# First attention of a two-block network: running sums of probabilities kept in a bank, three score banks, one wide reciprocal, second head's parts and a Fourier table moved later

## The reference

```
def one_block(qblk):
    s = einsum('bqhgd,bkhd->bhgqk', qblk, k) * scale
    p = softmax(s, axis=-1)
    return einsum('bhgqk,bkhd->bqhgd', p, v)
...
yb = blocked_attention(q, k_all, v_all)
y = concatenate([ya * silu(a_gate), yb * silu(b_gate)], axis=-1)
return y @ w_out
```

## Time and profile before

| | us |
|---|---|
| median of 3 runs | 4290.86 (4288.06 to 4292.45) |
| the profiled execution | 4291.51 |
| its span | 4289.7 |
| PE / PEld busy | 4061.0 / 3106.1 |
| DVE / ACT / POOL busy | 2073.7 / 1321.8 / 1532.8 |
| attention and its tail, about 360 to 649 us | 289 |

### The profile page before, as it was taken

The page is one execution under the profiler, slowest core; times in us unless marked ns, Lnnn a source line. Parts: engine busy times, 40 slices in busy tenths (PEclk is TensorE's granted clock), DMA queues, the critical chain, the costliest instruction groups (busy, mean ns, idle before and its releaser), DMA issues.

```text
span 4289.7 us, 49866 instructions
## 1 busy us (share of the span) xinstructions
PE 4061.0 (95%) x19447; PEld 3106.1 (72%) x19447; DVE 2073.7 (48%) x2300; ACT 1321.8 (31%) x1996; POOL 1532.8 (36%) x882
## 2 busy tenths in 40 slices
PE   7998998899999998899999999999999899999998
PEld 5776774457777774578888788876766578888886
DVE  4264883865676775561543233324454654323322
ACT  3123550222222221231332232234455533223222
POOL 0535770111111111122444444434454544444443
PEclk8999999999999999899999999999999999999999
DMA  6110005331122114741233333322000032333333
GB/s 231 38 40 20 1 1 207 128 133 63 66 80 74 70 68 164 179 141 49 89 93 98 98 98 94 102 79 73 22 25 26 16 118 93 98 98 95 96 99 106
DMA packets 118854, 372.15 MB, mean 87 GB/s; under 512 B 18020, under 2 KB 33695, under 8 KB 114912
## 3 DMA queue, kind: packets, MB, share of 16 engines
q1 hardware_dynamic: 98960, 296.38, 22.1%
q0 software_dynamic: 12800, 59.50, 3.9%
q10 hardware_dynamic: 6928, 13.96, 0.9%
HBM read 329.37 MB, written 38.06 MB: 86 GB/s over the span
## 4 chain that ended last, share of the span: by engine, by line
PE 65%; issue 15%; DVE 9%; POOL 6%; DMA 2%; ACT 2%; SPq 1%; POOLq 0%; ACTq 0%; DVEq 0%
PE banks L276 22%; PE banks L3218 6%; POOL w_parts L261 6%; PE banks L1344 6%; PE banks L291 5%; PE banks L696 5%; PE banks L1719 4%; PE banks L3292 2%; PE banks L3321 2%; PE banks L1001 1%; PE banks L3308 1%; PE banks L1700 1%; DMA w_ring<-in_weights 1%; PE banks L1014 1%; PE banks L1750 1%
## 5 line engine op out<-in xcount | busy, mean ns | idle before, releaser
L261 POOL TENSOR_TENSOR w_parts<-w_ring,w_parts 128x1024 fp32r<-128x1024 f32 x344 | 842.7, 2451 | 1089.4 <-ACT w_parts L254 1088.9
L276 PE MATMUL banks<-x_high,w_parts 128*128 128x512 f32 x2944 | 911.5, 390 | 0.0
L254 ACT ACTIVATE w_parts<-w_ring 128x1024 fp32r<-128x1024 f32 x344 | 364.6, 1060 | 1283.6 <-PE banks L276 1274.9
L276 PEld LDWEIGHTS banks<-x_high,w_parts 128*128 128x128 f32 x2944 | 552.7, 188 | 116.6 <-issue 2.1
L276 PE MATMUL banks<-x_low,w_parts 128*128 128x512 f32 x1472 | 572.7, 389 | 0.0
L276 PE MATMUL banks<-hidden_high,w_parts 128*128 128x512 f32 x1600 | 482.9, 392 | 6.0 <-POOL w_parts L261 6.0
L3426 DVE TENSOR_TENSOR_SCAN arena<-arena,flags 128x128 f32<-128x128 f32 (+3 forms) x192 | 248.6, 1308 | 250.5 <-ACT arena L3367 248.5
L276 PEld LDWEIGHTS banks<-hidden_high,w_parts 128*128 128x128 f32 x1600 | 302.6, 189 | 71.0 <-POOL w_parts L261 6.8
L3107 DVE TENSOR_TENSOR hidden_high<-banks,gate_temps 128x512 f32 (+1 forms) x88 | 60.8, 691 | 571.9 <-PE banks L276 571.7
L276 PEld LDWEIGHTS banks<-x_low,w_parts 128*128 128x128 f32 x1472 | 276.3, 188 | 59.3 <-issue 1.9
L1344 PE MATMUL banks<-parts_b,w_ring_low 128*128 128x512 f32 x896 | 304.7, 407 | 13.5 <-DVE resid_low L394 9.7
(11 more groups left out here) (478 smaller groups left out, 6832.2 us busy)
## 6 DMA issues: line engine op xcount, KB each, us to landing
w_ring<-in_weights SPq DMA_DIRECT2D x488, 512.0 KB, 3.6
arena<-in_hy_dft SPq DMA_DIRECT2D x11, 1536.0 KB, 6.2
s_cl<-arena POOLq DMA_DIRECT2D x4, 1152.0 KB, 5.4
resid<-in_xT ACTq DMA_DIRECT2D x2, 2048.0 KB, 26.2
resid<-in_xT POOLq DMA_DIRECT2D x2, 2048.0 KB, 12.7
arena<-in_fn_seq POOLq DMA_DIRECT2D x1, 4096.0 KB, 24.6
resid_spill<-resid POOLq DMA_DIRECT2D x1, 4096.0 KB, 12.7
s_e<-arena POOLq DMA_DIRECT2D x4, 1024.0 KB, 5.0
```

What stands on the lines that cost most here:

```text
L254: nc.scalar.activation(WP[:, g % 2, 0, :], WR[:, (g % RING) * TILE:(g % RING + 1) * TILE], ACT.Identity).then_inc(w_hi, 1)
L261: nc.gpsimd.tensor_tensor(WP[:, g % 2, 1, :], WR[:, (g % RING) * TILE:(g % RING + 1) * TILE], WP[:, g % 2, 0, :].bitcast(F32), ALU.subtrac ...
L276: mm = nc.tensor.matmul(PS[:, bank + h // H, :], w[a][:, k % KB, :], srcs[b][:, k, at + h:at + h + H], start=(first and i + q == 0), stop= ...
```

## The change

- The running sum moves from the SBUF tile `ACCP` to bank 3; only the last of a half's nine sums writes `ACCP`. Scores use three banks (i % 3) and wait for the exponentials of block i - 3.
- `denominator(g)` is one product of ones x `ACCP` (128x512) into bank 4, at s = 3; `spread` and `inverse` are gone. `divided(g - 1)` moves from s = 4 to s = 3 and begins with a reciprocal of the whole bank, 128x512, in place.
- The second head's high parts are made behind blocks 25 (keys) and 28 (values), its low parts behind blocks 26 and 29. The clearing of `SHIFT[1]` on GpSimd moves behind block 2; the first half's scores wait for one `a_sh` count less.
- ScalarE does one exponential of a single column ahead of its wait for the pooling part.
- `turned` counts on a semaphore of its own.
- The parameters' loads come ahead of the Fourier table, and the table is issued when the first f32 tile of the output projection is done.

```
-    a_hi, a_lo, a_mx, a_top, a_rc, a_sh = (sem("a_" + x) for x in ("hi", "lo", "mx", "top", "rc", "sh"))
+    a_hi, a_lo, a_mx, a_top, a_tt, a_sh = (sem("a_" + x) for x in ("hi", "lo", "mx", "top", "tt", "sh"))
...
             def scores(i):
-                if i == 3:
-                    p.wait_ge(pme, 4)
-                if i >= 4:
-                    p.wait_ge(a_p, i - 3)
-                out_ = PS[:, i % 4, :]
+                if i >= 3:
+                    p.wait_ge(a_p, i - 2)
+                out_ = PS[:, i % 3, :]
...
             def denominator(g):
                 p.wait_ge(a_ad, KBL * (g + 1))
                 p.wait_ge(a_top, 4 * min(g + 3, HALVES))
-                if g:
-                    p.wait_ge(a_o, 2 * g)
-                for t in range(4):
-                    mm = nc.tensor.matmul(PS[:, 4, t:t + 1], ACCP[g % 2][:, t * P:(t + 1) * P], ONES[:, 0:1],
-                                          start=True, stop=True)
-                mm.then_inc(a_dn, 1)
-            def spread(g):
-                p.wait_ge(a_rc, g + 1)
                 nc.tensor.matmul(PS[:, 4, :], ONES[:, :], ACCP[g % 2], start=True, stop=True).then_inc(a_dn, 1)
...
@@ act
             queries_high(0)
+            nc.scalar.activation(FLAG[:, 2:3], ONES[:, 0:1], ACT.Exp)
             a.wait_ge(pme, 4)
             values_high(0)
...
-                if i == 0:
+                if i == 25:
                     keys_high(1)
+                if i == 28:
                     values_high(1)
...
@@ dve, summed(i)
                 if b == 1:
-                    if g >= 2:
-                        v.wait_ge(a_dn, 2 * (g - 1))
-                    nc.vector.tensor_tensor(acc, PROB[(i - 1) % 3], PROB[i % 3], ALU.add).then_inc(a_ad, 2)
+                    if g:
+                        v.wait_ge(a_ad, KBL * g)
+                    nc.vector.tensor_tensor(PS[:, 3, :], PROB[(i - 1) % 3], PROB[i % 3], ALU.add).then_inc(a_ad, 2)
                 elif b > 1:
                     v.wait_ge(a_ad, i)
-                    nc.vector.tensor_tensor(acc, acc, PROB[i % 3], ALU.add).then_inc(a_ad, 1)
+                    if b == KBL - 1 and g >= 2:
+                        v.wait_ge(a_dn, g - 1)
+                    nc.vector.tensor_tensor(acc if b == KBL - 1 else PS[:, 3, :], PS[:, 3, :], PROB[i % 3],
+                                            ALU.add).then_inc(a_ad, 1)
...
             def divided(g):
-                v.wait_ge(a_dn, 2 * g + 2)
+                v.wait_ge(a_dn, g + 1)
+                link(nc.vector.reciprocal(PS[:, 4, :], PS[:, 4, :]))
                 v.wait_ge(a_o, 2 * g + 1)
...
                 if s == 3 and g:
-                    inverse(g - 1)
-                if s == 4 and g:
                     divided(g - 1)
...
@@ pool
-            g_.wait_ge(pme, 4)
-            nc.gpsimd.memset(SHIFT[1].bitcast(F32), 0.0).then_inc(a_sh, 1)
             values_low(0, 3)
             for i in range(BLOCKS):
                 prob_low(i)
+                if i == 2:
+                    g_.wait_ge(a_sh, 2)
+                    nc.gpsimd.memset(SHIFT[1].bitcast(F32), 0.0).then_inc(a_sh, 1)
                 if i == 3:
                     queries_low(1)
-                if i == 5:
-                    keys_low(1, 5)
-                if i == 8:
-                    values_low(1, 6)
+                if i == 26:
+                    keys_low(1, 7)
+                if i == 29:
+                    values_low(1, 8)
...
@@ HyPrep.pool
+            S5Prep.params(g)
+            wait_sums(g, EvOut.st, 3)
             g.dma_start(ar(0, 8192, "p (i b t) -> p i b t", i=2, b=8),
                         ins["fn_seq"].rearrange("i (b p) t -> p i b t", p=P)).then_inc(seq_in, 16)
-            S5Prep.params(g)
```

More of the change, by code:

```diff
@@ L948, in parts_made @@
     def parts_made(g):
-        return (2, 4)[g] if g < 2 else g + 5
+        return 2 if g == 0 else g + 3 if g < 4 else g + 5
     def top_bank(g, t):
@@ L987, in turned @@
                     p.wait_ge(a_sh, g + 2)
-                nc.tensor.transpose(PS[0:4, 6, 384:512], TOP[g % 2], IDENT[:, :]).then_inc(a_mx, 1)
+                nc.tensor.transpose(PS[0:4, 6, 384:512], TOP[g % 2], IDENT[:, :]).then_inc(a_tt, 1)
             def scores(i):
@@ L1002, in scores @@
                 if b == 0:
-                    p.wait_ge(a_sh, g + 3)
+                    p.wait_ge(a_sh, g + 3 if g else 2)
                 nc.tensor.matmul(out_, MINUS, SHIFT[g % 2], start=False, stop=True).then_inc(a_s, 1)
@@ L1009, in values @@
                 if b == 0:
-                    p.wait_ge(a_lo, 3 if g < HALVES // N_KV else 6)
+                    p.wait_ge(a_lo, 3 if g < HALVES // N_KV else 8)
                     if g:
@@ L1062, in pe @@
                 values(2 * n + 1)
-                if s == 4 and g:
-                    spread(g - 1)
                 if s == 2 and ahead:
@@ L1067, in pe @@
             denominator(HALVES - 1)
-            spread(HALVES - 1)
         def act(a, link):
@@ L1091, in act @@
                     a.wait_ge(a_ad, i - 2)
[L1092 removed]
+                nc.scalar.activation(PROB[i % 3], PS[:, i % 3, :], ACT.Exp, scale=SCALE0)
                 if i >= 3:
                     a.wait_ge(a_pv, i - 2)
[L1095 removed]
+                nc.scalar.activation(PPARTS[0][i % 3], PS[:, i % 3, :], ACT.Exp, scale=SCALE0).then_inc(a_p, 1)
                 if i % KBL == 0 and i // KBL + 1 < HALVES:
                     queries_high(i // KBL + 1)
[L1098 removed]
+                if i == 25:
                     keys_high(1)
+                if i == 28:
                     values_high(1)
@@ L1112, in top @@
             def top(g, t):
-                v.wait_ge(a_mx, 5 * g + t + 1)
+                v.wait_ge(a_mx, 4 * g + t + 1)
                 nc.vector.reduce_max(TOP[g % 2][:, t:t + 1],
@@ L1118, in shift @@
             def shift(g):
-                v.wait_ge(a_mx, 5 * g + 5)
+                v.wait_ge(a_tt, g + 1)
                 v.wait_ge(a_sh, g + 2 if g else 1)
@@ L1144, in gated @@
                 nc.vector.tensor_tensor(mixed_part(g), PS[:, 7, :], BG[:, g * H:(g + 1) * H], ALU.mult).then_inc(a_o, 1)
-            def inverse(g):
-                v.wait_ge(a_dn, 2 * g + 1)
-                link(nc.vector.reciprocal(PS[:, 4, 8:12], PS[:, 4, 0:4]))
-                nc.vector.tensor_tensor(ACCP[g % 2].rearrange("p (t n) -> p t n", t=4),
-                                        IDENT[:, :].unsqueeze(1).broadcast_to([P, 4, P]),
-                                        PS[:, 4, 8:12].unsqueeze(2).broadcast_to([P, 4, P]),
-                                        ALU.mult).then_inc(a_rc, 1)
             def divided(g):
-                v.wait_ge(a_dn, 2 * g + 2)
+                v.wait_ge(a_dn, g + 1)
+                link(nc.vector.reciprocal(PS[:, 4, :], PS[:, 4, :]))
                 v.wait_ge(a_o, 2 * g + 1)
@@ L1181, in dve @@
                 if s == 3 and g:
-                    inverse(g - 1)
-                if s == 4 and g:
                     divided(g - 1)
-            inverse(HALVES - 1)
             gated(HALVES - 1)
```

## The result

The changed kernel takes 4258.48 us (median of four runs, 4256.75 to 4261.16) against 4289.46 us for the kernel before (four runs too): ratio 0.9928, 95% interval 0.9911 to 0.9946, 31 us less. The forecast was 25 less, 4266; the measured time lies in the range 4249 to 4281.

What follows compares the result with a forecast made beforehand. It took a slow first half and a steady rhythm with VectorE nearly as full as TensorE to bound the attention; -9.5 - 11.6 - 2.4 + 0 - 1.5 = -25.0 us from 4291.5 gave 4266.5 (4266), range 4249 to 4281.

Steps and rivals of the forecast that it cites:

- The collision, and the sum's price in a bank: Attention sums: VectorE and GpSimd hold each other up reading SBUF; sums reading a bank cost 0.70 us, not 0.67 to 3.25.
- Rival D: Attention: sums still wait for GpSimd wherever they stand, the reciprocal is added; a half takes 24.5 us, total 4304; chance 0.06.
- Steady halves: Ten attention halves: TensorE's own 19.8 us plus 0.9 waiting for VectorE's chain, 20.7 each; -11.6 us (bounds -20 to 0).
- The two-input sum: Sum of a half's first two blocks, both read from SBUF, written to a bank: 0.68 us, up to 1.76 when colliding.
- Second head's parts: Attention: second head's keys and values, moved to blocks 26 and 29, add 1 us to the ten halves.
- First half: Attention's first half: exp table load earlier, second head's copies and subtractions gone; -9.5 us (bounds -11 to -7).
- Last half and tail: Attention's end: last half -2.4 us, tail up to the output projection's first tile 0 (bounds -2 to +2).
- a last half without waits: Attention's last half: TensorE's work alone sets its length, 15.3 us instead of 17.8, -2.4.
- Fourier table: Output projection: 4 MB load issued after the first tile, next weights land in 7.3 us; -1.5 us (bounds -7 to +1).
- they still meet: Output projection: table and next tile's weights, released by the same event, share bandwidth; weights land in 7.3 us, not 8.59.
- Rival C: Output projection: queues take equal turns, so the Fourier table's move pays in full, -5.6 us, total 4262; chance 0.11.
- Three banks at nothing: Attention scores: three banks instead of four cost nothing, as the exponentials are done at least 1.5 us ahead.

Runs made afterwards that it cites:

- e4: The changed kernel with the running sums in the SBUF tile `ACCP` again, all else kept; ratio 1.0006 to the kernel before.
- e11: The changed kernel with the fourth maxima step early, the projection's first tile started ahead and a half's first sum as copy plus add; 4248.12 us, ratio 0.9901.
- e1: The changed kernel with the old order of loads behind the attention (Fourier table first, no wait); ratio 0.9951 to the kernel before.
- e10: The changed kernel with the output projection's first f32 tile started before the attention's last half is divided; ratio 0.9926 to the kernel before.
- e15: The kernel before with only the second head's high and low parts moved behind blocks 25 to 29; ratio 0.9982.
- e3: The changed kernel with the second head's high and low parts made in the first half again; ratio 0.9942 to the kernel before.
- e7: The changed kernel with the fourth maxima step ahead of step 2's value blocks, and `turned` and `denominator` between step 3's score blocks; ratio 0.9916 to the kernel before.
- e2: The kernel before with only the loads' order changed: parameters first, Fourier table when the first f32 tile is done; ratio 0.9988.
- e6: The kernel before with scores in three banks, waiting for the exponentials of block i - 3, and nothing else; ratio 0.9999.
- e5: The changed kernel with the old narrow `denominator`, `inverse` and `spread` back, sums still in the bank; ratio 0.9924 to the kernel before.
- e13: e11 with the old narrow denominators in place of the wide reciprocal; ratio 0.9931 to the kernel before.
- e14: The kernel before with the parameters' loads ahead of the Fourier table, the table issued right behind them without a wait; ratio 1.0001.

## Why the prediction was right

The forecast was 25 us less and 31 were measured, inside the range. The mechanism of the steady halves came as laid out. The total is near partly by luck: the attention gained 21.5 us where 23.5 were forecast, and the output projection 8.1 where 1.5 were, by a step that was wrong.

- *The collision, and the sum's price in a bank.* 0.70 forecast, 0.69 measured, and e4 shows it as the cause. Rival D was priced at 24.5 us a half; e4 took 23.7.
- *Steady halves.* 20.7 forecast, 20.88 measured, by the chain that was named: sum 8 before the exponentials of block 1, `gated` before the value blocks. TensorE's own work was put at 19.8; e11, where no VectorE wait is left to see, runs 19.90. The two-input sum was mis-sized: 0.68 was the likely value and 1.76 the bound, and it is 1.77 on average. In the kernel before it mostly started just after GpSimd's low part had ended (at 493.94 us, behind one that ended at 493.87); now it starts 0.12 us after GpSimd has begun the low part of block 0, and so it collides in nearly every half. Of the Trainium skill's rule on it ("SBUF — State Buffer", section "Who interferes with whom": two SBUF inputs contend with a GpSimd instruction that reads SBUF) the trace bears out the direction; the estimate of 1.96 us from it is exceeded by the most seen, 3385 ns. That one began at 436.28 us, beside three low parts in a row on GpSimd (435.33 to 439.11 us), which had queued behind the second head's values subtraction (L1186, 2.96 us from 432.40).
- *Second head's parts.* 1 us forecast for their new place; 1.67 in half four of the changed kernel, where the collision of 3385 ns falls, and 0.45 in e1. Half two takes 0.57 us more than a steady half as well (21.45), which the prediction had at nothing.
- *First half.* -9.5 forecast, -11.1 measured. The last value block was laid out to end near 392.8 and ends at 393.21. The 1 us kept for a clock drop was not needed: the clock stays at 1.00 where it was 0.93 and 0.84. In e10 the clock did drop once (0.93 from 372 to 395 us), and the first half was 24.05 us long all the same. The attribution was one-sided: I gave nearly all to the place of the parts, and it does give 8.5 us alone (e15), but e3 takes 7.8 without it.
- *Last half and tail.* -2.4 forecast, -0.8 measured, and by the prediction's own cut all of it lies in the tail. The last half was to take TensorE's own 15.3 us; it takes 17.75 against 17.37 before. TensorE is busy 16.08 us of it and idle 1.67: 0.87 behind `gated`, 0.16 and 0.64 behind GpSimd's low parts. That step, a last half without waits, failed. The tail was put at 7.9 us and takes 7.18, because TensorE waits 1.88 us for the last sum and not 2.7. And the first tile behind it takes 1.76 us more, a price for which the prediction has no term; it is not always paid, as e7, with the same reciprocal, runs that tile in 14.02 us.
- *Fourier table.* -1.5 forecast; e2 gives -5, the output projection's mean length -5.8. The step that failed is "they still meet": the table's packets start when the weights are nearly in. The share was misread too: 76.1 against 27.4% is the mean of 656 to 664 us, where the weights' queue carried earlier loads up to 659.6 us and then nothing, and the weights in question had no packet before 666.64. While both queues moved in that kernel, the shares were 51.9 and 47.9% (667 to 671 us). That agrees with the Trainium skill's equal turns between queues ("DMA: Bandwidth & Descriptors", section "Queues, rings and completion order"), which the prediction had set aside. Rival C had the size (-5.6), but for the wrong reason in the changed kernel: while the weights moved there was hardly anything to take turns with, 0.12 MB against 0.52.
- *Three banks at nothing.* Right (e6).

The two profiled executions differ by 30.3 us in span, 5.3 more than forecast: 1.6 in the first half, 6.6 in the output projection and 0.6 behind it, less 2.1 in the ten halves and 1.6 in last half and tail; the rest is rounding. Some 2 us of the output projection are its own spread.

## What to carry to other kernels

When VectorE and GpSimd both read SBUF, look at the spread of a group and not at its mean: 669 to 3249 ns for one shape is a collision, and moving one operand of a running sum into a bank ends it for both engines. An operation added to an engine with idle time is not free because the engine is idle somewhere: lay out the chain from the last input it gets to the next thing it releases, and move the input sooner (the fourth maxima step) before you shorten the operation. A large load released by the same event as a small urgent one did no harm here, as it was not in flight already (weights in after 3.90 us); issued 13 us ahead, on a queue in full flow, it did (8.59 us). And when you read a queue's share, take the stretch in which the load in question has packets, not one around it.

## What the runs showed of the hardware that was not expected

- The f32 tile of 32 matmuls mostly takes 13.94 to 14.02 us or 15.71 (seen more rarely: 14.42 to 14.74, and 15.90 to 17.07), and which rounds of the output projection take the longer time differs from execution to execution: one to four of its eight in every kernel here. Every longer tile of the 14 kernels has a stretch at granted clock 0.50 in it and no other tile has one; the time added is half of that stretch, to 0.1 us. Most stand behind a wait for weights of 3.66 to 5.59 us (7.87 to 8.59 where the table is in flow) or behind the attention's tail; in before, e4 and e6 one tile of 14.42 to 14.74 stands behind no wait, but behind small products (in before L1420, L490 and L484, 745.76 us). A wait alone doesn't decide it: one of 3.67 us was followed by 15.71 (e5), another of 3.67 by 14.02 (e13), and one of 5.29 by 14.00 (e4). What does stays open. It makes this stage's length spread over 6 us in kernels that don't differ there.
- The stage's own times repeat far better than the program's: a steady half is 20.87 to 20.93 us in e1, e3, e10 and the changed kernel, and the attention of before, e2, e6 and e14 is 279.59 to 279.72 us long, while single runs of the kernel before span 4283.5 to 4298.0 us.
- Beside a queue in full flow, another queue's load starts late: the first packet of the second tile's weights comes 3.65 to 3.67 us after their issue in before, e1 and e14, and 0.97 to 1.14 us after it in e2 and the changed kernel.
- A two-input VectorE sum that ran beside three GpSimd instructions in a row took 3385 ns, five times its own 680.
